# A hybrid recurrent decoder step on one core: several stages reordered (C's 4th power on GpSimd, 320 columns in layer 2, level 5, final states, sums, the heads' end)

## What is computed

```python
# layer 0: RG-LRU | HGRN2 (8 heads each), one input and one output projection
z = rmsnorm(x) @ w_in_e                      # 6 splits of 1024
xc = causal_dwconv(xa, a_conv, conv_a_w, conv_a_b)
ha, hl = rg_lru(xc, ...)                     # gates, then linear_scan
out_a = ha * gelu(ga)
out_b, S = hgrn2(q, fz, v, gb, ...)          # gated linear attention
x = x + concatenate([out_a, out_b]) @ w_out_e
x = conv_ffn(x)
# layer 1: S5, diagonal complex SSM in 64 groups of 16 channels and 64 states
u = rmsnorm(x) @ w_in_c
sr, si = complex_scan(a, B u)                # states
y = Re(C s) + d_skip * u
x = x + (gelu(y) @ w_glu_v) * sigmoid(gelu(y) @ w_glu_g)
x = conv_ffn(x)
y = rmsnorm(x)
# conv_ffn: x + (gelu(dwconv3(h @ w_up)) * (h @ w_gate)) @ w_down, D_FF = 5504 = 43 * 128
```

## Time and profile before

| | us |
|---|---|
| median of 3 runs | 2815.04 (2814.56 to 2816.85) |
| the profiled execution | 2814.19 |
| its span, first to last instruction | 2812.4 |
| PE busy | 2732.0 (97%) |
| DVE busy | 1587.4 (56%) |
| ACT busy | 1164.8 (41%) |
| POOL busy | 384.3 (14%) |
| mean granted clock of PE | 0.987 of full speed |

### The profile page before, as it was taken

How to read it: one execution, slowest core, us unless ns; L and a number is a source line. 1 busy time by engine, 2 the same in 40 slices (tenths; PEclk the granted TensorE clock), 3 DMA queues, 4 the chain that set the end, 5 groups by cost and what they waited for, 6 DMA issues and landing times.

```text
span 2812.4 us, 54094 instructions
## 1 busy us (share of the span) xinstructions
PE 2732.0 (97%) x19961; PEld 2693.5 (96%) x19961; DVE 1587.4 (56%) x2639; ACT 1164.8 (41%) x1508; POOL 384.3 (14%) x527
## 2 busy tenths in 40 slices
PE   7999999999999999999999997999999999999997
PEld 7999999999999999999999986999999999999996
DVE  7556665546554455655555557565554555455554
ACT  5544445334433333435554333443333334333333
POOL 1333333221000000060002440210000000000011
PEclk9999999999999999999999999999999999999998
DMA  6444444455544555445444421445555554555543
GB/s 176 130 126 129 132 134 130 119 143 155 142 141 141 147 142 146 135 135 144 141 140 134 142 85 37 136 134 147 148 144 148 149 149 142 149 153 147 145 140 93
DMA packets 739213, 382.97 MB, mean 136 GB/s; under 512 B 13560, under 2 KB 734756, under 8 KB 739140
## 3 DMA queue, kind: packets, MB, share of 16 engines
q1 hardware_dynamic: 722352, 365.34, 45.7%
q10 hardware_dynamic: 14228, 9.31, 1.1%
q0 software_dynamic: 2560, 7.29, 1.0%
HBM read 373.31 MB, written 8.57 MB: 136 GB/s over the span
## 4 chain that ended last, share of the span: by engine, by line
PE 86%; DVE 6%; issue 3%; ACT 3%; POOL 1%; ACTq 1%; DMA 0%; DVEq 0%; SPq 0%; POOLq 0%
PE banks L1549 28%; PE banks L1550 28%; PE banks L1551 27%; ACT wh L484 1%; DVE wl L997 1%; DVE SB L1219 1%; PE banks L1688 1%; PE banks L1614 0%; DVE CT L1165 0%; DVE X L1236 0%; POOL BX L408 0%; DVE m L1433 0%; DMA xin<-in_x_sample 0%; DVE m L1431 0%; PE banks L1697 0%
## 5 line engine op out<-in xcount | busy, mean ns | idle before, releaser
L997 DVE TENSOR_TENSOR wl<-raw,wh 128x1024 fp32r<-128x1024 f32 x708 | 889.3, 1257 | 920.6 <-ACT wh L484 919.7
L1549 PE MATMUL banks<-h,wh 128*128 128x336 f32 (+1 forms) x3648 | 1158.6, 318 | 9.3 <-DVE h L1007 3.6
L1550 PE MATMUL banks<-h,wh 128*128 128x336 f32 (+1 forms) x3648 | 1150.2, 315 | 0.0
L1551 PE MATMUL banks<-h,wl 128*128 128x336 f32 (+1 forms) x3648 | 1147.7, 315 | 0.0
L484 ACT ACTIVATE wh<-raw 128x1024 fp32r<-128x1024 f32 x708 | 748.7, 1058 | 934.1 <-PE banks L1551 920.4
L1549 PEld LDWEIGHTS banks<-h,wh 128*128 128x128 f32 x3648 | 687.9, 189 | 16.1 <-issue 6.3
L1550 PEld LDWEIGHTS banks<-h,wh 128*128 128x128 f32 x3648 | 687.3, 188 | 1.7
L1551 PEld LDWEIGHTS banks<-h,wl 128*128 128x128 f32 x3648 | 687.3, 188 | 0.0
L1549 PE MATMUL banks<-act,wh 128*128 128x336 f32 (+1 forms) x1888 | 598.5, 317 | 11.4 <-DVE X L1236 2.9
L1550 PE MATMUL banks<-act,wh 128*128 128x336 f32 (+1 forms) x1888 | 595.3, 315 | 0.0
L1551 PE MATMUL banks<-act,wl 128*128 128x336 f32 (+1 forms) x1888 | 593.5, 314 | 0.0
(11 more groups left out here) (357 smaller groups left out, 1722.1 us busy)
## 6 DMA issues: line engine op xcount, KB each, us to landing
raw<-in_w_up SPq DMA_DIRECT2D x172, 512.0 KB, 4.0
raw<-in_w_gate SPq DMA_DIRECT2D x172, 512.0 KB, 4.0
raw<-in_w_down SPq DMA_DIRECT2D x160, 448.0 KB, 3.8
raw<-in_w_in_e SPq DMA_DIRECT2D x96, 512.0 KB, 3.8
raw<-in_w_out_e SPq DMA_DIRECT2D x32, 512.0 KB, 4.1
raw<-in_w_down SPq DMA_DIRECT2D x32, 512.0 KB, 4.1
raw<-in_w_in_c SPq DMA_DIRECT2D x16, 512.0 KB, 3.8
raw<-in_w_glu_v SPq DMA_DIRECT2D x16, 512.0 KB, 4.1
```

The source lines that it names most:

```text
L997: v.tensor_tensor(wl[:, j % RING, :], raw[:, j % RING, :], wh[:, j % RING, :].bitcast(F32), ALU.subtract) \
L1549: pe.matmul(out, whi, hi, start=first and k == 0, stop=False)
L1550: pe.matmul(out, whi, lo, start=False, stop=False)
L1551: ins = pe.matmul(out, wlo, hi, start=False, stop=last and k == kn - 1)
```

## The change

1. DVE takes level 5 in step 7, between the copies of the last convolution rows and the convolution.
2. The end of the last head: PE runs channels 0 to 6 of wout's tiles 0 and 1 first, with the key transposes in the middle of tile 0 and the products into BO in the middle of tile 1, then channel 7 of both; the norm product goes into tile 2, the state products behind tile 3. ACT does GELU first, the key copies and OB, W after the rounding of tile 4. The state stores move behind step 3, DVE's state chain into step 3.
3. Sums into X go ahead of the split in wout, down and glu; on ACT, glu's sigmoid ahead of the rounding.
4. The second tile of up and win waits for 15 low halves at its start, for the 16th before its last channel.
5. C's 4th power is made by POOL into a buffer of its own (C4) behind the last BX, with a table of d_skip; ACT spreads C4 into CT4 after its state copies; DVE adds the table to bank 6 during win, before ACT makes K5. The scan's last two quarters are one.
6. The nine final-state transposes fill three banks and are copied by three instructions; PE waits for them after glu 4, and the FFN states follow there.
7. In layer 2's FFN the gate and down tiles leave out 16 columns, META, instead of 14; the up tiles stay at 14.

```diff
@@ ScalarE @@
-            for t, stages in enumerate(((0, 2), (1, 5), (6,), (), (), (), (), ())):
+            for t, stages in enumerate(((2,), (5,), (6,), (1,), (), (), (), ())):
+                if t == 0:
+                    gate_made(HEADS - 1)
                 if t == 1:
+                    keys_taken(HEADS - 1)
                     output_taken(HEADS - 1)
                 for j in stages:
                     end_of(HEADS - 1, j)
+                if t == 4:
+                    states_stored(HEADS - 1)
                 round_tile(first, t // 4, t % 4)
...
-            e.wait_ge(bx_used, STEP)
+            e.wait_ge(k_made, 1)
+            e.wait_ge(c4_made, 1)
             for g in range(2):
                 ins = sc.activation(K5..., bank[6]..., ACT.Copy, scale=masks[:, g:g + 1])
...
+            e.wait_ge(ct4_zero, 1)
+            for g in range(2):
+                rowsl = slice(g * P5, (g + 1) * P5)
+                for r in range(2):
+                    ins = sc.activation(CT4[rowsl, :, r, :]..., C4[rowsl, r]..., ACT.Copy)
+            ins.then_inc(ct4_made, 1)
...
                 for j in range(4):
-                    round_tile(ph, i, j)
                     if j % 2:
                         e.wait_ge(used, ph.tile(i, j) + 1 + CREDIT)
                         sc.activation(GS[:], bank[j][:, 0:T], ACT.Sigmoid).then_inc(gsig, 1)
+                    round_tile(ph, i, j)
+                    if j % 2:
                         hi_of_x(ph, i, j, COL["g_ffn"] + DC, i * 2 + j // 2)
...
-            for s in range(9):
-                e.wait_ge(fs_t, s + 1)
-                sc.activation(io5o[:, s, :], BM[s % 2][0:2 * PAIRS, 0:P], ACT.Copy).then_inc(fs_c, 1)
-            e.wait_ge(fs_c, 9)
+            for b, (s0, n) in enumerate(((0, 4), (4, 4), (8, 1))):
+                e.wait_ge(fs_t, b + 1)
+                sc.activation(io5o[:, s0:s0 + n, :]..., TB[b][0:2 * PAIRS, 0:n * P], ACT.Copy).then_inc(fs_c, 1)
+            e.wait_ge(fs_c, 3)
@@ GpSimd @@
+            for r in range(2):
+                times_power(gp, st, C0, 3, r, C4[:, r], bq[:], OF_C)
+                st.then(gp.tensor_tensor(C4[:, r], C4[:, r], bq[:], ALU.add))
+            gp.tensor_tensor(skip5[:], eye5..., prm[:, COL["d_skip"]:COL["d_skip"] + 8]..., ALU.mult).then_inc(skip_made, 1)
+            gp.memset(sq[:, 0:1], 0.0).then_inc(c4_made, 1)
+            e.wait_ge(c4_made, 1)
             e.wait_ge(bx_used, STEP)
             e.wait_ge(ms_done, 3)
@@ VectorE @@
-                    if j in LV_HALF:
+                    if j in LV_HALF and j != 8:
                         level(LV_HALF[j])
...
                         v.tensor_copy(ncva[:, 1:1 + NS, :, ds(i, 1)]..., XAs[:, :, LS:LS + 3])
+                        level(LV_HALF[8])
                         e.wait_ge(ct, n)
...
-            for t, stages in enumerate(((5, 2), (6,), (), (), (), (), (), ())):
+            for t, stages in enumerate(((5,), (6,), (), (2,), (), (), (), ())):
+                if t >= 4:
+                    multiplied(first, t // 4, t % 4)
+                    add_to_x(first, (t - 4) // 2, t % 2, t % 4, WOUT_BANK[t - 4])
                 split_tile(first, t // 4, t % 4)
...
                         for j in range(4):
+                            if j >= 2:
+                                add_to_x(ph, i, j - 2, j)
                             split_tile(ph, i, j)
                             if j >= 2:
-                                add_to_x(ph, i, j - 2, j, g, norm_next)
+                                low_of_sum(i, j - 2, g, norm_next)
...
+                    if (i, j) == (3, 2):
+                        e.wait_ge(bx_used, STEP)
+                        e.wait_ge(skip_made, 1)
+                        first = bank[6][:, 0:8 * C5].rearrange("p (j c) -> p j c", c=C5)
+                        v.tensor_tensor(first, first, skip5[:], ALU.add).then_inc(k_made, 1)
...
-            for u in range(4):
-                scan_quarter(u)
+            scan_pairs(0, 1)
+            scan_pairs(1, 2)
+            scan_pairs(2, 4)
@@ TensorE @@
+            def early(ph, t, then):
+
+                e.wait_ge(split, ph.tile(0, t) + 1 + CREDIT)
+                for k in range(HEADS - 1):
+                    channel(k, t)
+                    if k == 3:
+                        then(HEADS - 1)
...
             ph = PH["wout"]
+            e.wait_ge(evac, ph.group(0, 0) + BANK_CREDIT - 2)
+            early(ph, 0, keys_turned)
+            e.wait_ge(evac, ph.group(0, 0) + BANK_CREDIT - 1)
+            early(ph, 1, lambda i: end_of(i, 0))
+            e.wait_ge(act_lo, 2 * HEADS - 1)
+            for t in range(2):
+                last_of(ph, t)
             e.wait_ge(evac, ph.group(0, 0) + BANK_CREDIT)
-            for t in range(8):
+            for t in range(2, 8):
                 half = None
-                if t == 0:
-                    half = lambda: keys_turned(HEADS - 1)
-                if t == 1:
+                if t == 2:
                     half = lambda: end_of(HEADS - 1, 5)
                 if t == 4:
                     e.wait_ge(act_lo, 2 * HEADS)
...
-                if t < 2:
-                    end_of(HEADS - 1, t)
+                if t == 3:
+                    end_of(HEADS - 1, 1)
...
                             if first and j < 2:
-                                e.wait_ge(h_lo, split_h - (DC // 2 if j == 0 else 0))
-                            tile(..., None, l * DEAD)
+                                e.wait_ge(h_lo, split_h - (DC // 2 if j == 0 else 1))
+                            tile(..., None, l * (DEAD if j < 2 else META),
+                                 (lambda: e.wait_ge(h_lo, split_h)) if first and j == 1 else None)
...
-                            tile(ph, i, j, kn, from_act(k0), ph.bank(j % 2), j < 2, j >= 2, None, l * DEAD)
+                            tile(ph, i, j, kn, from_act(k0), ph.bank(j % 2), j < 2, j >= 2, None, l * META)
...
-            e.wait_ge(k_made, 1)
             e.wait_ge(x5a, 8)
...
             for s in range(9):
-                if s >= 2:
-                    e.wait_ge(fs_c, s - 1)
-                pe.transpose(BM[s % 2]..., fin5[:, s]..., ident[:]).then_inc(fs_t, 1)
-            e.wait_ge(fs_c, 9)
+                ins = pe.transpose(TB[s // 4]..., fin5[:, s]..., ident[:])
+                if s % 4 == 3 or s == 8:
+                    ins.then_inc(fs_t, 1)
+            glu(4)
+            e.wait_ge(fs_c, 3)
             e.wait_ge(sf_in, 16 * 6 * 2)
             past_turned(1, range(0, 4))
-            glu(4)
+            glu(5)
```

More of the change, by code:

```diff
@@ L1860, in win @@
                     if first and j < 2:
-                        e.wait_ge(h_lo, 3 * DC - (DC // 2 if j == 0 else 0))
-                    tile(ph, i, j, 8, from_h(8 * (j % 2)), ph.bank(j // 2), j % 2 == 0, j % 2 == 1)
+                        e.wait_ge(h_lo, 3 * DC - (DC // 2 if j == 0 else 1))
+                    tile(ph, i, j, 8, from_h(8 * (j % 2)), ph.bank(j // 2), j % 2 == 0, j % 2 == 1,
+                         before_last=(lambda: e.wait_ge(h_lo, 3 * DC)) if first and j == 1 else None)
                     if first and j == 1:
@@ L1929, in _ @@
             for s in range(9):
[L1930 to L1933 removed]
+                ins = pe.transpose(TB[s // 4][0:2 * PAIRS, s % 4 * P:s % 4 * P + P], fin5[:, s].rearrange("p r q -> p (r q)"), ident[:])
+                if s % 4 == 3 or s == 8:
+                    ins.then_inc(fs_t, 1)
+            glu(4)
+            e.wait_ge(fs_c, 3)
             e.wait_ge(sf_in, 16 * 6 * 2)
             past_turned(1, range(0, 4))
[L1936 removed]
+            glu(5)
             past_turned(1, range(4, 6))
[L1938 removed]
+            with e.Fori(6, 8) as i:
                 glu(i)
```

105 lines of the change are left out of this document (57 added, 48 removed).

## The result

The changed kernel takes 2765.3 us (median of 4 runs, 2763.98 to 2766.21) against 2814.8 for the kernel before in the same session: ratio 0.9821, 95% interval 0.9808 to 0.9833, 50.4 us of 2815.0. In a second session the same code came to 0.9828 (0.9815 to 0.9842), 48.4 us. Forecast were 44.0 us and 2771.0. The direction and most mechanisms held. The gain was 4 to 6 us larger than the sum: on 2815.0 the first ratio gives 2764.6 us, just under the low end of the range (2765), and the second 2766.6, just above it. One term brought nothing at all, and two (3 and 7) were too small.

What follows compares the result with a forecast made beforehand. TensorE (PE) was busy 97% of the span, so only its idle stretches, low-clock stretches and streamed columns could move the time. Seven numbered parts summed to 44.0 us off 2815.0, giving 2771.0; range 2765 to 2783.

Steps and rivals of the forecast that it cites:

- Term 1: Heads 1 to 7: level 5 ahead of the convolution ends PE's waits for AT; gain 4.0 us.
- term 3: First tiles of up and win ask later for the last low half, 3.6 us; sums into X precede the split, 2.9.
- term 7: Layer 2's gate and down tiles: 320 columns instead of 322 shorten 4128 matmuls; gain 3.0 us.
- rival A: Heads' end: the clock falls again at the eight-column products, or ACT brings W late; 2775 us, chance 0.15.
- Term 2: Heads' end: reordered work keeps PE busy and the clock up, 32.3 us becoming 21.9; gain 10.4.
- Rival E: Waits are only passed on, so parts 1 and 3 bring a third; 2778 us, chance 0.03.
- Term 4: S5: the scan starts 6.0 us earlier with DVE's work moved to POOL, joined quarters save 1.7; gain 7.7.
- rival B: S5: splits hold POOL for their whole length, st_in comes 2.4 us late; 2773.4 us, chance 0.10.
- Term 5: Final states: nine transposes in three banks go without waiting for ACT and the clock holds; gain 8.0 us.
- Term 6: End of glu: sigmoid and sums first cut PE's idle from 3.5 to 1.6 us and the clock holds; gain 4.4.
- Rival C: After glu: the clock falls in spite of the shorter idle, 2.5 us lost; 2773.5 us, chance 0.10.
- Rival D: Layer 2's narrower matmul runs slower than the 322-column one; at 15 ns a matmul 2836 us, chance 0.02.

Runs made afterwards that it cites:

- b_sums: The kernel before with the sums into X ahead of the split in wout and down alone: 0.9949, 14.4 us faster.
- a_spread: The changed kernel with the last-step sample products of each head spread, two behind each of tile 1's first four channels: 0.9807 of the kernel before, 2759.4 us.
- a_spread_lv5back: The changed kernel with the sample products spread and level 5 back behind the convolution: 0.9822 of the kernel before.
- a_lv5back: The changed kernel with level 5 back behind the convolution: 0.9831 of the kernel before.
- best: The changed kernel with sample products spread and S5's start edited (K5 copies, last U, C's power and skip table moved): 0.9794 of the kernel before, 2755.7 us.
- a_noend: The changed kernel with the heads' end as before: 0.9872 of the kernel before, 36.0 us faster than it.
- after_again: The changed kernel once more, unaltered, in a second session: 0.9828 of the kernel before.
- widths1: The changed kernel with layer 2's up tiles 324 columns from column 12, gate 318 from 16, down 326 from 10: gate matmuls took 147.5 ns.
- b_first: The kernel before with only the second tile of up and win waiting for the 16th low half just ahead of its last channel: 0.9986, 3.9 us.
- widths2: The changed kernel with layer 2's gate tiles 320 columns from column 14, down 328 from 8: gate matmuls took 148.1 ns.
- widths3: The changed kernel with layer 2's gate tiles 320 columns from column 12, down 316 from 16: gate matmuls took 147.7 ns.

## Why the prediction was right in direction and short in size

The steps that failed are terms 1, 3 and 7. Terms 3 and 7 were mis-sized and carried the gain past the range: term 3 gave 6.5 us, and b_sums, a part of it, brings 14.4 (10.7 to 18.3) by itself; term 7 gave 3.0 and measured 4.3 to 5.0. Term 1 failed in its mechanism and hid some of that excess: its stretch lost 1.1 us where 3.4 were forecast.

- **Term 1 was wrong.** "Gain 4.0, bounds 2.0 and 4.0": alone it gives 1.4 us, with an interval that holds zero, and the changed kernel's heads lost 1.1. The waits went (4.9 us, a_spread against a_spread_lv5back) but were paid back at 1.4 to 1.6 us a fall, in three to five heads where the kernels before had one or two. The prediction had the narrow products in rival A alone, for the heads' end, and looked for no fall inside the heads. The lower bound had to hold a clock loss, since one head of the kernel before already had such a fall.
- **Term 2 was right** in its whole chain: 21.6 us for 21.9. Rival A did not happen: the clock held, W was 0.27 late. That was in part luck: of the ten profiles of kernels with this heads' end three (a_lv5back, a_spread, best) have a fall between 486 and 508 us, and their stretch to ncva took 99.9 to 100.7 us instead of 98.8 to 99.7. (The stretch gained 1.1 more ahead of the last h tile's end, where the kernel before waited 0.7 for AT at full clock.)
- **Term 3 was too small.** The row of 2.9 was read from PE, where a matmul's modelled end lies 0.16 us behind the next one's start, so every wait is shown too short and a short one not at all. The loads' rows say 9.8 for what I priced at 6.5, and another 1.7 lay in layer 2, where nothing was priced. Rival E did not happen: the stretch gained more than the waits shown, not a third of them.
- **Term 4 was right, but its profiled execution unlucky**: from the last BX to fin 6.0 us gained of 7.7. Kernels with the same S5 code gained 9.7 (a_lv5back), 7.9 (a_noend), 7.4 (a_spread) and 7.4 (after_again). The clock at the first read-ins makes the difference of the first profile, whose scan began 1.6 to 2.0 us later than in the others. a_lv5back's last 2 us lie behind the scan (87.6 us from its end to fin, 89.0 to 89.9 in the others), and their cause is not shown. The join of the quarters was sized well: the scan took 24.4 instead of 26.4, 2.0 for 1.7. POOL was nearer to the limit than I had it, as these rows of the changed kernel show (POOL and DVE):

```profile
1628.57 1.93 POOL L400 TENSOR_TENSOR C<-C,AP 128x512 f32<-128x512 f32 x1
1631.59 2.16 POOL L999 TENSOR_TENSOR C<-C,bq 128x512 f32<-128x512 f32 x1
...
1627.34 2.23 DVE L1029 TENSOR_TENSOR wl<-raw,wh 128x1024 fp32r<-128x1024 f32 x1 [1.34 <-ACT wh L485]
1631.02 1.58 DVE L1029 TENSOR_TENSOR wl<-raw,wh 128x1024 fp32r<-128x1024 f32 x1 [1.44 <-ACT wh L485]
```

  Three operations beside splits took 0.87 more each. The group took 10.1 us (1624.17 to 1634.27) for 7.4 without collisions and 11.2 by rival B, and st_in ended 5.9 us after PE's start of S5, where I had 5.3: 0.6 late, not 2.4. The Trainium skill (SBUF — State Buffer, "SBUF: two separate sides") has whoever starts first keep the shared port pair for its whole instruction, with the other blocked. The trace agrees that the later one waits: POOL's sum of 1631.59 began while a split had 1.01 us to go and took 0.87 more than the sum of 1627.20 (1.29), and the split of 1627.34, begun behind that sum, took 2.23 instead of 1.23. Rival B charged a split's whole 1.26 for each collision; only the rest of it counted.
- **Term 5 was right**: 0.90 us for nine transposes, the clock 1.00 behind them; 8.5 + 1.3 - 0.9 and some 0.6 for the other four is 8.3, for 8.0.
- **Term 6 was right**: 3.5 to 1.73 of idle and no fall behind it (clock 1.00 from 1825 to 1835, 2.7 not lost) is 4.5, for 4.4. Rival C did not happen here, but it did in two of the eleven profiles of kernels with this glu: a_spread and widths1 have a clock of 0.89 from 1815 to 1830 us, and from fin to the last NCF a_spread took 1.6 us more than the changed kernel.
- **Term 7 was too small**: 4.3 to 5.0 us for 3.0. I took the slope between 336 and 322 columns from two windows, one of which also held the hidden waits for X, and carried it on to 320. From 322 to 320 it was 0.6 ns a column in gate tiles. Rival D did not happen.
- Against the forecast the table has -4.5 for the heads, +0.8 for their end, +3.2 for layer 1's FFN and win, -1.7 for S5, +4.2 from the final states on (columns and hidden waits) and +1.6 at the very end, where b_sums gained 1.3 too: +3.6 in the profiled pair, more by the medians. "Below 2767.9 would need a gain that I don't see" was the failing sentence of the range: the highs were bounded by idle rows that do not show whole waits.

## What to carry to other kernels

Price a wait of PE by the rows of its weight loads as well as by those of its matmuls. Here the matmuls' rows were too low by some 0.16 us a wait; the loads' rows were near for the waits at tile starts (9.8 for 9.0 to 9.7 gained) and too high for AT (6.0 us in seven waits, worth 4.9). Short waits at every bank may show in neither, but in the matmuls per microsecond of a long window. Removing an idle gap is worth nothing where the clock then falls elsewhere: look for stretches of narrow matmuls, and mix them among wide ones before counting the gap as gained. Two edits that take the same lateness away are priced together, by one run with each alone.

## What the runs showed of the hardware

- PE's clock fell to 1.2 GHz with PE busy without a gap, half a microsecond behind a stretch of narrow matmuls (some 3 us: blocks of 128, 80 and 16 columns, then 16 instructions of eight), in up to five of seven heads; with the narrow ones set among matmuls of 336 columns it did so at none of 21 ends of heads. The Trainium skill (TensorE: Matmul & The Clock Gate, "What's actually happening") ties the clock to how busy PE has been. Here rows at full busy time fell, so busy time as the profile prints it does not tell whether the clock will hold.
- An idle of 2.5 us at the start of S5 was followed by a clock of 0.50 in the changed kernel's first profile and by full clock in the kernel before (1.00 from 1663.6 to 1670). Eight other profiles with the changed kernel's S5 code began the scan 1.6 to 2.0 us earlier, so one profile of an edit here can be off by that much.
- In the profiles of four of the sixteen kernels and repeats (a_lv5back, b_first, widths2, widths3) layer 1's FFN had a stretch of some 300 us in which matmuls of 336 columns came every 155.5 ns instead of 153.3, with no wait and at full clock; a window each of the changed kernel and of a_lv5back:

```profile
1300.00:1400.00 100.00, 100.00 (x654) 1.00 0.49 139
```

```profile
1300.00:1400.00 100.00, 100.00 (x645) 1.00 0.51 144
```

  It costs 3 us, and its cause is open. It is as large as several of the differences measured here, so single parts of this kernel under 3 us are better read from their own stretch than from the total.
